# Moving the grouped heads' own max pair ahead of the step's scores

## The reference

```python
xn = rms_norm(h, norm_in); proj = xn @ w_in            # q, k, v, gates, latents
# group A: 8 query heads of 64 on 2 key/value heads ("grouped heads")
# group B: 4 heads with keys of 96 and values of 128, from low-rank latents
def one_block(qblk):                                   # softmax attention, all 2048 keys
    s = einsum('bkgqd,bksd->bkgqs', qblk, k) * scale
    p = softmax(s, axis=-1)
    return einsum('bkgqs,bksd->bkgqd', p, v)
y = concat([y_a * silu(a_g), y_b * silu(b_g)])
h = h + y @ w_out
```

## The kernel before, in words

| steps | scores | max pair | its unit |
|---|---|---|---|
| 0 to 4 | a | a (L1249) | second group-A unit of this iteration |
| 5 to 12 | a | b (L1251) | group-B unit of this iteration |
| 13 to 15 | a | a (L1249) | first group-A unit of the next iteration |
| 16 to 23 | b | a (L1249) | group-A units of the next iteration |

## Time and profile before

### The profile page before, as it was taken

How to read it: one execution, slowest core, us unless ns; L and a number is a source line. 1 busy time by engine, 2 the same in 40 slices (tenths; PEclk the granted TensorE clock), 3 DMA queues, 4 the chain that set the end, 5 groups by cost and what they waited for, 6 DMA issues and landing times. The chain is left out here.

```text
span 1633.4 us, 36760 instructions
## 1 busy us (share of the span) xinstructions
PE 1527.7 (94%) x13138; PEld 879.8 (54%) x13138; DVE 1164.3 (71%) x1616; ACT 1052.2 (64%) x1377; POOL 580.1 (36%) x504
## 2 busy tenths in 40 slices
PE   6889999999991899999999999999999999949999
PEld 3445555555550465666566566656665665624444
DVE  6665464646554989988998899889889988642332
ACT  7544444444440888888888888888888888841110
POOL 0100000000000565665666566656656665700000
PEclk9999999999995999999999999999999999979999
DMA  8476755675547333232233324322323333179894
GB/s 297 138 160 124 169 139 129 138 173 116 120 105 176 128 79 67 60 81 64 72 82 80 64 61 97 80 64 61 83 63 75 78 81 67 38 199 245 240 236 116
DMA packets 354846, 189.70 MB, mean 116 GB/s; under 512 B 174480, under 2 KB 335760, under 8 KB 354800
## 3 DMA queue, kind: packets, MB, share of 16 engines
q1 hardware_dynamic: 329232, 173.31, 43.6%
q10 hardware_dynamic: 24672, 14.88, 3.6%
q0 software_dynamic: 896, 0.93, 0.4%
HBM read 119.16 MB, written 40.93 MB: 98 GB/s over the span
## 5 line engine op out<-in xcount | busy, mean ns | idle before, releaser
L1122 POOL TENSOR_TENSOR p_pl<-p_p,p_ph 128x512 f16<-128x512 f32 x384 | 502.0, 1314 | 403.7 <-ACT p_ph L1158 345.0
L1173 DVE TENSOR_REDUCE p_part<-p_mx 128x2 f32<-128x1024 f32 x384 | 468.4, 1220 | 86.5 <-PE p_mx L1249 68.2
L1149 ACT ACTIVATE p_p<-p_st 128x1024 f32<-128x1024 f32 x384 | 391.0, 1019 | 124.4 <-PE p_st L1281 66.7
L822 PE MATMUL p_ring<-p_w_hi,p_xT 128*128 128x512 f16 (+3 forms) x1536 | 387.6, 340 | 17.4 <-DVE p_xT L652 13.8
L1158 ACT ACTIVATE p_ph<-p_p 128x1024 f16<-128x1024 f32 x336 | 355.2, 1057 | 18.4
L1201 DVE TENSOR_TENSOR p_pl<-p_p,p_ph 128x512 f16<-128x512 f32 x384 | 325.1, 847 | 9.3 <-ACT p_ph L1158 8.5
L822 PE MATMUL p_ring<-p_w_lo,p_xT 128*128 128x512 f16 (+3 forms) x768 | 261.4, 340 | 0.0
L822 PEld LDWEIGHTS p_ring<-p_w_hi,p_xT 128*128 128x128 f16 x1536 | 151.7, 99 | 136.7 <-DVE p_xT L652 9.1
L1313 PE MATMUL p_acc<-p_vas,p_ph 128*128 128x129 f16 x2048 | 207.9, 221 | 0.0
L1314 PE MATMUL p_acc<-p_vas,p_pl 128*128 128x65 f16 x2048 | 201.0, 193 | 0.0
L1313 PEld LDWEIGHTS p_acc<-p_vas,p_ph 128*128 128x128 f16 x2048 | 180.6, 97 | 36.3 <-issue 14.3
(11 more groups left out here) (117 smaller groups left out, 1950.2 us busy)
## 6 DMA issues: line engine op xcount, KB each, us to landing
p_vbs<-scratch_vb SPq DMA_DIRECT2D x16, 1028.0 KB, 6.4
p_xin<-in_x SPq DMA_DIRECT2D x16, 512.0 KB, 6.2
p_xcol<-in_x_cols SPq DMA_DIRECT2D x16, 512.0 KB, 6.0
scratch_g<-p_g SPq DMA_DIRECT2D x16, 512.0 KB, 4.6
p_kb<-scratch_kb SPq DMA_DIRECT2D x32, 256.0 KB, 5.3
p_xr<-in_x SPq DMA_DIRECT2D x16, 512.0 KB, 4.7
out<-p_res SPq DMA_DIRECT2D x16, 512.0 KB, 3.1
p_gt<-scratch_g ACTq DMA_DIRECT2D x14, 512.0 KB, 4.8
```

The source lines that it names most:

```text
L822: last = pe.matmul(ring_t[:, 0:w], a, b, start=(k == 0 and m == 0), stop=(k == len(steps) - 1 and m == len(terms) - 1))
L1122: pool.tensor_tensor(pl[:, s % NP, 1, :], p32[:, s % N32, QB:], ph[:, s % NP, 1, :], ALU.subtract).then_inc(s_lop, 1)
L1149: act.activation(p32[:, s % N32, :], st[:, s % 2, :, :].rearrange("p a b -> p (a b)"), ACT.Exp, scale=scale).then_inc(s_exp, 1)
L1173: dve.tensor_reduce(part[:, e // MPAIRS % 3, 2 * c:2 * c + 2], mx[:, :, :], AX, ALU.max).then_inc(s_red, 1)
```

## The change

TensorE's order is altered in the steps whose scores and whose max pair are both of kind a (`lone`: steps 0 to 4 and 13 to 15). There the max pair is issued ahead of the scores, so the order over steps becomes max pair, scores, P V products. In the other 16 steps the order stays scores, max pair, P V products. No instruction is added or removed, and no other engine's or queue's program is altered.

```diff
             def body(i, first, last):
                 v = -PV_CARRY
                 for s in range(HALF):
+                    lone = UNITS[s // STEPS][1] == "a" and UNITS[(s + LEAD) // MPAIRS % 3][1] == "a"
+                    ahead = not (last and s + LEAD >= HALF)
+                    if ahead and lone:
+                        max_pair(i, s + LEAD, False)
                     scores(i, s, first)
-                    if not (last and s + LEAD >= HALF):
+                    if ahead and not lone:
                         max_pair(i, s + LEAD, False)
                     for _ in range(PV_HALVES[s]):
                         if not (first and v < 0):
```

## The result

The changed kernel takes 1650.4 us (median of 4 runs, 1649.56 to 1650.79) against 1634.2 for the kernel before (median of 4 runs): a ratio of 1.0104, 95% interval 1.0072 to 1.0135. It is slower by 1.0%, as forecast; 1654.1 was predicted. The profiled execution took 1650.79 us, its span is 1648.9.

A forecast was written before the change was run, and what follows sets the result against it. TensorE sets the pace, VectorE has little to spare; TensorE's max pairs wait for VectorE's reductions through one shared PSUM tile. 9.0 + 8.1 + 1.7 = 18.8 us on 1635.3 gave 1654.1 us, range 1641 to 1662.

The forecast's parts named there:

- The mechanism and the ordinary iterations: Where runs of moved steps begin, the max pair waits for VectorE's reduction, scores queued behind: 9.0 and 8.1 us.
- 0.60 + 0.54: Loss per iteration in us: 0.60 at step 0, 0.54 at step 13, each times 15 iterations.
- The switch of shape: Ahead of max pairs, 128 to 64 rows: 0.10 us, move worth 0; bounds 6.4 us gained or lost.
- the test that I named: Steps 1 to 4 take as long as before, 2.0 and 2.7 us; wrong if 0.1 shorter or longer by more.
- The cheap switch: Rival at moved pairs: array empties at once after a short product, 6.4 us less, 1647.7 us; chance 0.17.
- The first iteration: Without P V products ahead of scores 0, the pair waits and scores start 1.73 later: 1.7 us, ends 0 and 1.7.
- The low parts: Rival: VectorE's low parts collide with GpSimd's in steps 0 to 3, at most 8 us more, taken 1658; chance 0.12.
- One sign that I named: In the profile after, the grouped pair's total wait for the reduction rises from 45 us to well over 60.

The follow-up runs named there:

- The kernels with one half of the change: Against the kernel before (attention phase 919.8 us): only steps 0 to 4 moved, phase 931.4 us; only steps 13 to 15 moved, 927.7 us.
- the short reduction: VectorE reduces 256 of 512 columns per product: attention phase 899.0 us with the old order, 903.7 us with the whole change on top.
- the last kernel of the study: Whole change on top of the kernel with VectorE's reciprocal right behind the step's reduction (attention phase 910.9 us): phase 934.7 us.
- the opposite move: Against the kernel before, no pair moved ahead; max pairs of steps 14 to 17 put behind the P V products: attention phase 940.8 us against 919.8.

## Why the prediction was right, and which term was off

*The mechanism and the ordinary iterations* came out as put down. From the second to the last iteration, scores 0 are 56.07 apart before and 57.20 after, 1.13 more where 0.60 + 0.54 = 1.14 was forecast; 15 x 1.13 = 17.0 against 17.1. Behind pair 23, pair 0 starts after 1.70 (forecast 1.71) and P V 0 after 2.92 (2.91). Pairs 16 and 17 start 3.46 and 5.67 behind pair 15 (forecast 794.25 and 796.47 less 790.80, 3.45 and 5.67). The kernels with one half of the change and the one with a run that begins at step 2 show that it is the beginning of a run that costs; the short reduction shows that it is the wait.

*The switch of shape* costs the same behind a short product: from the last P V product of step 0 to pair 1 it takes 0.16 (819.24 to 819.40), where the next product of such a row comes after 0.06, so 0.10 as behind scores. Steps 1 to 4 kept their length, which was the test that I named. I had spoken of a 65-column product there; the P V products of steps 0 to 4 are in fact those of the group-B unit before, which end with 129 columns. A pair that follows a 65-column product without waiting is pair 15 in the last kernel of the study:

```profile
850.88 0.22 PE L1314 MATMUL p_acc<-p_vas,p_ph 128*128 128x129 f16 x1
...
852.02 0.41 PE L1250 MATMUL p_mx<-early 64*128 64x512 f16 x2
```

P V 14 and the switch take 1.15 there, P V 14 alone 1.06 (789.68 - 788.28 - 0.34), so 0.09. The cheap switch is out. The Trainium skill, TensorEngine Tiling (Array Packing), Key Properties, speaks of a drain at a change of tiling mode; these rows agree, and show it as long after 65 or 129 columns as after 512.

*The first iteration* is the term that was mis-sized: 1.7 in the sum, 19.8 - 17.0 = 2.8 measured, outside the ends of 0 and 1.7 that I gave. Two things were left out. Scores 0 came 2.03 later instead of 1.73 (21.98 against 19.95 behind the first pair). The moved pair and these scores after the change:

```profile
530.56 0.62 PE L1249 MATMUL p_mx<-early 64*128 64x512 f16 x2 [1.41 <-DVE p_part L1173]
531.11 0.61 PE L1280 MATMUL p_st<-early 128*128 128x512 f16 x1
```

I took the 0.34 from pair to scores from a row at 2.4 GHz, but at that place the clock stood at 1.2 (granted clock 0.50 from 530 to 534 us), and 0.55 was due. The pair also started 0.15 behind the end of the reduction (529.19 + 1.22 = 530.41), not 0.06. The other 0.8 came later, in steps in which TensorE waited longer than before and its clock fell. Granted clock is the number behind the GpSimd column in these two rows, of 546 to 550 us, before and after:

```profile
546.00:550.00 4.00, 3.76 (x47) 2.26 (x44) 4.00 (x4) 3.00 (x4) 2.52 (x3) 1.00 0.09 24
```

```profile
546.00:550.00 4.00, 4.00 (x39) 2.56 (x37) 3.18 (x3) 1.43 (x3) 1.91 (x2) 0.67 0.02 4
```

In the timeline of TensorE after the change, this is a max pair that waited 1.25 us, and scores a little later:

```profile
544.64 0.62 PE L1251 MATMUL p_mx<-p_kb_m,p_qb_m 96*128 96x512 f16 x2 [1.25 <-DVE p_part L1173]
...
547.37 0.63 PE L1281 MATMUL p_st<-early 128*128 128x512 f16 x1
547.80 0.63 PE L1280 MATMUL p_st<-early 128*128 128x512 f16 x1
```

Behind the wait TensorE fell from 2.4 to 1.2 GHz for a time: those scores are 0.43 apart in place of 0.21. That it fell because of the wait is argued from the order of events; no kernel tested it alone, and how the 0.8 is shared between the clock and the waits stays open. In the kernel with steps 0 to 4 moved the clock was 1.00 in this stretch and 0.50 in 534 to 538, and the start still cost 11.7 - 9.05 = 2.6, or 2.3 without one later iteration that took 0.3 longer than the others.

*The low parts* did collide more often (mean 871 ns from 600 to 1500 us, 844 before from 600 to 1480), but no pair of steps 1 to 4 waited for it, so that rival added nothing here. By the trace it is what decided the opposite move.

*One sign that I named was wrong.* The total wait of the grouped pair in the list of waits did not rise "well over 60". After the change it reads:

```profile
PE p_mx L1249 <- DVE p_part L1173: 23.3, 42, 0.7
PEld p_mx L1249 <- DVE p_part L1173: 21.4, 42, 0.7
```

Before, the 45.2 us of 98 waits were the weight loader's, and much of that ran while the scores' last product was still streaming: the loader idles from its last load, not from the last product. What TensorE lost has to be read from starts, as in the working. The row of the products themselves, which the prediction did not look at, is nearer to it. Before the change it reads:

```profile
PE p_mx L1249 <- DVE p_part L1173: 4.8, 14, 0.3
```

It rose from 4.8 us in 14 places to 23.3 in 42, three in each of 14 iterations: pairs 0, 13 and 14, the places named, with 0.53, 0.69 and about 0.44 where 0.6 to 0.7 was given. The total of the loader's row is not a bill.

## What to carry to other kernels

When two engines pass one buffer back and forth, list what lies between two fills, not the order within a step: here a change of order cost only where a run of moved steps began, and the instruction that comes first there holds up all behind it for as long as the buffer is not free. A waiting instruction should stand behind work that needs nothing from it, not ahead; but that alone is no recipe, as the kernel with pairs 14 to 17 late shows, which lost 21 us. Before moving the engine that waits, look for what makes the other one late: here a reciprocal of 0.17 us that GpSimd waited for was worth 8.9 us.

## What was not expected of the hardware

Operations of VectorE on 4 columns took up to 1.08 us instead of 0.16 beside GpSimd's work. And a single wait of 1.25 us on TensorE, in a phase with little work, was followed by some 3 us at half clock, while waits of 0.4 to 0.7 us in the dense iterations, three in each, left it at 1.00 (690 to 1448 us).
